# Layer norm tails rebuilt around the next stage's first products, and the first expert weights split inside the routing chain

## The reference, cut down

```
mix = hybrid_mixer(x, w_in[l], ...)                 # x @ w_in (1024 x 3088), attentions, then y @ w_out (1024 x 1024)
x = layer_norm(ALPHA * x + mix, ln1_g[l], ln1_b[l])
ffn = (silu(conv(x @ w_up)[gate]) * conv(x @ w_up)[value]) @ w_down    # 2 x 2816 columns up, 2816 rows down
x = layer_norm(ALPHA * x + ffn, ln2_g[l], ln2_b[l])

def layer_norm(x, g, b):
    mu = x.mean(-1); var = square(x - mu).mean(-1)
    return (x - mu) * rsqrt(var + 1e-5) * g + b
```

## Time and profile before

| | |
|---|---|
| median of 3 runs | 3308.24 us (3307.53 to 3309.69) |
| profiled execution, its own time | 3307.87 us |
| its span, first to last instruction | 3306.1 us |
| PE busy | 2997.5 us (91%) |
| DVE busy | 2490.6 us (75%) |
| ACT busy | 1367.0 us (41%) |
| POOL busy | 453.8 us (14%) |
| mean granted PE clock | 0.941 |

### The profile page before, as it was taken

One profiled execution on the slowest core, in us unless ns is written; L12 is line 12 of the kernel. 1 busy time (PEld: TensorE's weight loads), 2 busy tenths in 40 slices (PEclk: granted clock), 3 DMA queues, 4 the chain that ended last, 5 costly groups with the idle time before them and its releaser, 6 DMA issues. The chain is left out here.

```text
span 3306.1 us, 40370 instructions
## 1 busy us (share of the span) xinstructions
PE 2997.5 (91%) x13932; PEld 2416.0 (73%) x13932; DVE 2490.6 (75%) x2714; ACT 1367.0 (41%) x1618; POOL 453.8 (14%) x252
## 2 busy tenths in 40 slices
PE   8987999989988999879978999995998969999995
PEld 6776888867766878757767888884765767888884
DVE  4566888565568995676958999996487658999996
ACT  1241211002311110064235777773336227777774
POOL 0111113211102123300000000002323000000001
PEclk9998999989988999989988999997999979999997
DMA  4243664322324663164229999994212339999993
GB/s 165 64 160 102 194 215 153 115 106 90 140 90 141 218 202 115 39 176 120 73 111 353 373 370 374 385 362 155 90 54 84 117 137 373 378 378 388 386 385 142
DMA packets 346507, 667.25 MB, mean 202 GB/s; under 512 B 21936, under 2 KB 138604, under 8 KB 338172
## 3 DMA queue, kind: packets, MB, share of 16 engines
q1 hardware_dynamic: 339612, 642.58, 55.5%
q0 software_dynamic: 6752, 22.81, 2.0%
HBM read 612.20 MB, written 53.13 MB: 201 GB/s over the span
## 5 line engine op out<-in xcount | busy, mean ns | idle before, releaser
L2702 DVE TENSOR_TENSOR expert_w_low<-expert_w_raw,expert_w_high 128x2048 fp32r<-128x2048 f32 x290 | 663.3, 2289 | 64.9 <-ACT expert_w_high L2663 64.7
L2663 ACT CAST expert_w_high<-expert_w_raw 128x2048 fp32r<-128x2048 f32 x290 | 554.9, 1914 | 181.3 <-PE bank L144 178.3
L142 PE MATMUL bank<-expert_w_high,expert_x_high 128*128 128x512 f32 x928 | 379.5, 409 | 5.4 <-DVE expert_w_low L2702 4.5
L144 PE MATMUL bank<-expert_w_high,expert_x_low 128*128 128x512 f32 x928 | 364.8, 393 | 0.0
L142 PE MATMUL bank<-first_XH,first_w_high 128*128 128x512 f32 x912 | 363.1, 398 | 1.1 <-DVE first_w_low L221 1.1
L143 PE MATMUL bank<-expert_w_low,expert_x_high 128*128 128x512 f32 x928 | 363.7, 392 | 0.0
L143 PE MATMUL bank<-first_XL,first_w_high 128*128 128x512 f32 x912 | 357.2, 392 | 0.0
L144 PE MATMUL bank<-first_XH,first_w_low 128*128 128x512 f32 x912 | 356.8, 391 | 0.0
L221 DVE TENSOR_TENSOR first_w_low<-first_w_raw,first_w_high 128x2048 fp32r<-128x2048 f32 (+2 forms) x100 | 302.8, 3028 | 3.4
L219 DVE CAST first_w_high<-first_w_raw 128x2048 fp32r<-128x2048 f32 (+2 forms) x100 | 119.8, 1198 | 173.3 <-PE bank L144 167.8
L2535 POOL DMA_INDIRECT expert_x_rows<-h_rows,slot_token x58 | 66.2, 1142 | 1266.8 <-PE bank L2568 862.5
(11 more groups left out here) (523 smaller groups left out, 6013.2 us busy)
## 6 DMA issues: line engine op xcount, KB each, us to landing
expert_w_raw<-in_moe_w_gate_dram SPq DMA_DIRECT2D x116, 1024.0 KB, 8.3
expert_w_raw<-in_moe_w_up_dram SPq DMA_DIRECT2D x116, 1024.0 KB, 13.9
expert_w_raw<-in_moe_w_down_dram SPq DMA_DIRECT2D x58, 1024.0 KB, 13.6
modulation<-in_moe_w_down_dram SPq DMA_DIRECT2D x58, 1024.0 KB, 13.9
ffn_mod_w<-in_ada_w_dram SPq DMA_DIRECT2D x48, 1024.0 KB, 5.0
first_w_raw<-in_w_up_dram SPq DMA_DIRECT2D x88, 512.0 KB, 6.4
first_w_raw<-in_w_down_dram SPq DMA_DIRECT2D x22, 1024.0 KB, 4.9
first_w_raw<-in_w_in_dram SPq DMA_DIRECT2D x20, 1024.0 KB, 5.1
```

The costliest lines, as they stand in the source:

```text
L142: nc.tensor.matmul(out, rounded(st[0]), rounded(mv[0]), start=start, stop=False)
L144: return nc.tensor.matmul(out, rounded(st[1]), rounded(mv[0]), start=False, stop=stop)
L2663: nc.scalar.copy(rounded(high[:, part_of(e, n), :]), weights.place(place)).then_inc(w_high, 1)
L2702: nc.vector.tensor_tensor(rounded(low[:, part_of(e, n), :]), weights.place(place), high[:, part_of(e, n), :], ALU.subtract).then_inc(w_spl ...
```

## The change

**Layer norm.** A class `RowNorm` replaces both tails. The mean and the sum of squares are now taken on ACT, each by one 1024-wide activation with an accumulator (L1056 and L1060 of the new file), with a small one for the negated mean between them (L1058). DVE does two 1024-wide scalar_tensor_tensor instructions per tile, which take in gain and bias. POOL does nothing in a tail.

**Order on PE.** `last_products` replaces `last_tiles`: the transposes of tiles 0 and 1 stand before the last two product tiles. Between and behind the transposes of tiles 2 and 3 stand the next phase's first products: in `output_norm_phase` the two jobs of up slot 0, in halves of 256 tokens (`up_job`), in layer 0's `ffn_phase` the four jobs of the first half-depth slot of the next projection (`first_value_job`). The next phase skips them, and both of its first slots are split already: high parts on ACT, low parts on DVE, inside the tail. Layer 1's `ffn_phase` has the new norm alone.

**Experts.** ACT writes the first slot's high part before the second small exponential. DVE writes the first low part before the wait for `ranked`, the second before the wait for `listed`, and the third behind the rows. The second half of the first rows is transposed into bank 7.

```diff
+def last_products(slots, tile, used, turn):
+    f, l = slots - 2, slots - 1
+    if f % Weights.RING == 0:
+        tile(f, 0)
+        tile(f, 1)
+        tile(l, 0, True)
+        tile(f, 2)
+        tile(l, 1, True)
+        tile(f, 3).then_inc(used, 1)
+        rest = l
+    else:
+        tile(f, 0)
+        tile(f, 1)
+        tile(l, 0, True)
+        tile(l, 1, True)
+        tile(l, 2)
+        tile(l, 3).then_inc(used, 1)
+        rest = f
+    turn(0)
+    tile(rest, 2, True)
+    turn(1)
+    tile(rest, 3, True)
...
+    def deviation(self, act, t):
+        x, at = self.G["X"][:, t, :], slice(t, t + 1)
+        act.wait_ge(self.summed, 2 * t + 2)
...
+        self.nc.scalar.activation(self.squares, x, ACT.Identity, accum_out=self.total[:, at]).then_inc(self.total_done, 1)
...
+        self.nc.scalar.activation(self.less_mean[:, at], self.total[:, at], ACT.Identity, scale=-1.0 / D).then_inc(self.mean_done, 1)
...
+        self.nc.scalar.activation(self.squares, x, ACT.Square, bias=self.less_mean[:, at], accum_out=self.square_sum[:, at]
...
+        self.nc.scalar.activation(self.std[:, at], self.square_sum[:, at], ACT.Sqrt, scale=1.0 / D, bias=self.G["eps_ln"][:, :]
```

In `output_norm_phase`, PE:

```diff
+            row_products(nc, pe, ps, weights, acts, product_done, lambda t: norm.turn(pe, t, turned))
+            norm.turn(pe, 2, turned)
+            pe.wait_ge(next_weights.split, 1)
+            pe.wait_ge(split.low, 4)
+            up_job(nc, G, next_weights, 0, slice(0, 2 * P))
+            norm.turn(pe, 3, turned)
+            up_job(nc, G, next_weights, 1, slice(0, 2 * P))
+            pe.wait_ge(split.low, 8)
+            for i in range(2):
+                up_job(nc, G, next_weights, i, slice(2 * P, 4 * P)).then_inc(next_weights.done, 1)
```

In `ffn_phase`, PE, where a next projection exists:

```diff
+                pe.wait_ge(next_weights.split, 1)
+                pe.wait_ge(split.low, 2)
+                first_value_job(nc, G, next_weights, 0)
+                norm.turn(pe, 2, turned)
+                pe.wait_ge(split.low, 4)
+                first_value_job(nc, G, next_weights, 1)
+                norm.turn(pe, 3, turned)
...
```

In the expert phase, DVE (the two functions run before the waits for `ranked` and `listed`):

```diff
+            chain.on_vector(dve, lambda: weight(Step(0), 0), lambda: weight(Step(0), 1))
             for half in range(2):
                 rows(None, half)
+            for n in range(2, PARTS):
+                weight(Step(0), n)
```

More of the change, by code:

```diff
@@ L1043, in row_products @@
         last.then_inc(weights.used, 1)
-    for s, t in last_tiles(slots):
-        pe.wait_ge(weights.split, s + 1)
-        tile(s, t)
+    last_products(slots, tile, weights.used, turn)
 def output_norm_phase(nc, l, G, weights, g_dram, b_dram, next_weights):
@@ L1098, in stats_of @@
[L1098 to L1105, removed]
@@ L1116, in _ @@
             for s in range(1, slots):
                 weights.split_slot(dve, s)
[L1118 to L1124 removed]
+            for t in range(2):
+                norm.residual(dve, t)
+                norm.centre(dve, t)
+                norm.scale(dve, t)
+            norm.residual(dve, 2)
+            split.low_parts(dve, 0)
@@ L1126, in _ @@
+            next_weights.split_low_dve(dve, 0)
+            norm.residual(dve, 3)
+            norm.centre(dve, 2)
+            norm.scale(dve, 2)
+            split.low_parts(dve, 1)
+            norm.centre(dve, 3)
+            norm.scale(dve, 3)
+            split.low_parts(dve, 2)
+            split.low_parts(dve, 3)
+            next_weights.split_low_dve(dve, 1)
         @block.scalar
         def _(act):
-            for t in range(TT):
-                act.wait_ge(var_done, t + 1)
-                nc.scalar.activation(std[:, t:t + 1], mv[:, t, 1:2], ACT.Sqrt, bias=G["eps_ln"][:, :]).then_inc(std_done, 1)
@@ L1131, in _ @@
-            split.high_parts(act)
-        @block.gpsimd
-        def _(pool):
-            pool.wait_ge(rows_loaded, 32)
-            for t in range(TT):
-                pool.wait_ge(scaled, t + 1)
-                nc.gpsimd.tensor_tensor(X[:, t, :], X[:, t, :], b_row[:, :], ALU.add).then_inc(shifted, 1)
+            norm.deviation(act, 0)
+            norm.deviation(act, 1)
+            act.wait_ge(weights.used, slots - 1)
+            next_weights.split_high(act, 0, None)
+            split.high_part(act, 0)
@@ L2449, in expert_phase @@
         down_bank = lambda c: ps[4 + c]
+        rows_bank = lambda first, half: ps[HIDDEN_BANK if first and half else X_BANK]
         block = ph.block()
```

282 lines of the change are left out of this document (155 added, 127 removed).

## The result

The changed kernel takes 3270.66 us (median of 4 runs, 3265.62 to 3272.11) where the kernel before takes 3307.89: a ratio of 0.9883, interval 0.9871 to 0.9895. Applied to the 3308.24 of the front that is 3269.5, half a microsecond under the range of 3270 to 3289 that was forecast: 38.7 us gained where 31 were forecast. By the two medians alone the gain is 37.2 us. The profiled execution is the fastest of the four (3265.6).

A forecast was written before the change was run, and what follows sets the result against it. PE bounds the stages, so time can come only from the seams where it waits. Gains 10 + 14.2 + 3 + 3.8 = 31 us off 3307.9 give 3276.9, with 0.4 for the median 3277.3; range 3270 to 3289.

The forecast's parts named there:

- I take 5 for each of the two tails, 10 together: Both output_norm tails: new norm and next phase's products moved into the tail; worked gain 5.3 us each, taken as 5.
- job j = 1: First product job left behind the first output_norm tail's barrier: to start at 329.1, after barrier, wait for taps and transposes.
- Half products: Next phase's 256-column products in the output_norm tails, priced at 0.12 us each, 72 of them ending at 324.6.
- rival 1: Output_norm tails: halves load-bound, 0.16 to 0.236 us instead of 0.12, 3.8 to 11 us more per tail; 3285 to 3299; 10%.
- the estimate of 0.216 us: Output_norm tails: load and half product not overlapped; 96 cost 9 us more per tail, total about 3296.
- Layer 0's ffn tail: New order, norm and moved products let PE start the second half-depth slot at 715.4, not 729.6: gain 14.2 us.
- The table load: Layer 0's ffn tail: ACT's 1.28 us load now stands between tile 0's squares and root; deviation 1.3 late, PE waits 0.7.
- Layer 1's ffn tail: Only the new norm: last low part ends at 708.9 against 711.9, gain 3 us.
- Experts: Two expert phases: gather 2.0 us late, but first products at 1748.5 against 1750.42; gain 1.9 us each, 3.8 together.
- Rival 2: Transfers or DVE late at the next phase's start, 2 to 4 us in each of three places: 3283 to 3289; 10%.
- Rival 3: PE's clock recovers earlier or does not fall at the barrier, 2.3 us in up to three seams: 3268 to 3274; 12%.
- Rivals 4 and 5: Tails lengthen by what next phases save, 3301 to 3310, 4%; PE stays at 1.2 GHz in up stage, 3315 up, 2%.

The follow-up runs named there:

- splits_behind_chain: Changed kernel, but in the expert phases DVE writes the first two low parts directly behind the routing chain, not inside it: 3269.65 us, ratio 0.9877.
- taps_inside: Changed kernel, but in both ffn phases PE turns the convolution's taps inside its first job, behind 12 of its 24 products: 3276.39 us, ratio 0.9898.
- busy_wait: Changed kernel with 12 more products, result unused, at the start of each ffn phase ahead of the wait for the taps: 3271.88 us, ratio 0.988.
- early_and_taps: Changed kernel with the next phase's slot 2 requested inside the tail and the taps turned inside PE's first job: 3261.12 us, ratio 0.9853.

## Why the prediction was wrong

- **The step that failed** is the size of "I take 5 for each of the two tails, 10 together": 6.5 and 7.7 in one profile, 6.8 and 7.0 in the other. That is 4.2 of the 6.1 us by which the seams of the first profile exceed the forecast of 31, and 3.8 of the 4.6 of the second. The mechanism was right. In the first tail, with 3.1 added to the times of the new profile, tile 2's transposes were put at 309.0 and stand at 305.19 + 3.1 = 308.3; the halves' end at 324.7, and it is 323.3; job j = 1 at 329.1, and it is 328.0. The first 0.7 comes from DVE: I added busy times, and neighbours overlap.

```profile
303.85 1.28 DVE L1079 SCALAR_TENSOR_TENSOR x_tokens<-mix_out_centred,mix_out_rstd,mix_out_b_row 128x1024 f32<-128x1024 f32 x1
305.05 1.28 DVE L261 TENSOR_TENSOR first_XL<-bank,first_XH 128x512 fp32r<-128x512 f32 x2
306.25 1.28 DVE L1071 SCALAR_TENSOR_TENSOR mix_out_centred<-x_tokens,mix_out_less_mean,mix_out_g_row 128x1024 f32<-128x1024 f32 x1
```

  Rows of 1.28 start 1.20 apart, and the earlier trace rows give only their length. The eight instructions from low part 0 to tile 2's norm take 7.2 us (297.86 to 305.05), where I had 7.8. Another 0.5 comes from tile 2's transposes, which give way to the half job after 1.3 us (305.19 to 306.48) and not 1.8, since the clock rose within them. And I rounded 5.3 down to 5. In the second tail of the first profile come another 1.2. Half of it is the kernel before, which took 0.6 longer over this tail than over the first. The other half is what is left of an earlier rise of the clock (24 half products in 3.5 us, against 4.1) and a shorter wait for the taps: PE was 1.7 us ahead of the first tail by its fifth product and lost 1.1 of it again, in part in a wait of 0.5 us for slot 2.

```profile
976.94 0.56 PE L142 MATMUL bank<-first_XH,first_w_high 128*128 128x256 f32 x1
980.41 1.03 PE L1088 MATMUL bank<-ident,x_tokens 128*128 128x128 f32 x8
993.76 0.44 PE L1358 MATMUL bank<-ident,ffn_small_rows 44*128 44x44 f32 x4 [3.68 <-DMA ffn_small_rows<-in_conv_b_dram]
```

- **Half products** at 0.12: measured 0.121 at full clock. The pair of load and product takes little more than half of 0.227, so the load lies beside the products, and rival 1 falls. With it falls the estimate of 0.216 us for a pair that does not overlap, worked out from the 107 ns of a load in the Trainium skill, "TensorE: Matmul & The Clock Gate", section "LDWEIGHTS (loading the stationary operand)".
- **Layer 0's ffn tail**: 14.2 forecast, 15.3 measured; the first product behind the barrier at 714.2 on the time axis of the kernel before (704.61 + 9.6), not 715.4. Same cause: the 15 us of DVE work from residual 2 to the last low part were summed by their lengths to 16. The table load stands where it was put, and PE waits 0.33 us behind it, not 0.7:

```profile
675.59 1.28 ACT L1063 ACT_TABLE_LOAD   x1
676.88 0.30 ACT L1063 ACTIVATE ffn_std<-ffn_square_sum,eps_ln 128x1 f32<-128x1 f32 x1
```

- **Layer 1's ffn tail**: 3 forecast, 3.2 and 3.3 measured. **Experts**: 3.8 forecast; 4.4, 3.2 and, alone, 3.6 measured. But one step in it was wrong in size: counted from the router's first row, the gather was issued 1.4 us later than before and its rows were turned 1.0 us later in the first phase of the first profile (1.0 to 1.7 in the four of both profiles), not 2.0. And the chain's waits were no good place for the low parts, as splits_behind_chain shows.
- **Rival 2** (transfers late at the next phase) was nearer than its 10%: I found "1 to 2 us of room" for up slot 2; there was none. PE waits 0.3 and 0.5 us for it in two of the four tails of the two profiles. What taps_inside and busy_wait let PE start earlier was lost there, until slot 2 was requested earlier. Projection slot 2 kept its room: DVE had split it at 714.08, and no row of PE there carries a wait. **Rival 3** (the clock rises earlier) shows in two of these four tails: the 11 intervals behind the taps take 4.0 and 4.2 us there, 4.8 and 4.9 in the others. But its price was worked out wrong: 2.3 us in one to three seams below 3277.3 is 3270.4 to 3275.0, not 3268 to 3274. **Rivals 4 and 5** did not come.
- **The range** ended at 3270 because only rival 3 led below the forecast; the sum itself, made of lengths that erred to the slow side, had no bound of its own downward. Both ways of reading the result lie within 0.7 us of that end.
- **Open**: how much of the second output_norm tail's 7.7 and 7.0 us is the change. Against the shorter execution of the old tail (1.6 us) they are 6.1 and 5.4, and the tails' excess over the 10 is 2.6 and 2.2 us. Why the clock rose earlier in one execution than in another is not shown.

## What to carry to other kernels

Sum what DVE does in a row by the distances between starts, not by the lengths of its rows: over a tail of 15 us the lengths were 1 us too long, always to the same side. When a seam is shortened, look at once for the transfer that is requested behind it: here two edits that each brought nothing, or lost 6 us, brought 9 together. Products of the next phase that need only half the rows fill the waits of a tail well; the norm and the splits alone did not move an output_norm tail. And profile the kernel before more than once: one of its seams differed by 1.6 us between two executions.

## What the hardware showed that was not expected

- Pauses of PE of 1.0, 1.5 and 1.6 us left its clock at the upper level (0.227 to 0.236 us a product of 512 columns behind them), as did the 2.81 of the earlier trace rows, whose transposes still take 1.09. Behind pauses of 3.7 to 4.4 us the lower level came, at once or after some products: the first 11 intervals took 4.0 to 4.9 us.
- How soon the clock rises again differs between executions of one program: the same 24 half products took 3.5 to 4.3 us in the two profiles of the changed kernel.
- POOL's low part of 2048 columns took 4.61 us beside DVE's work, and DVE's rows, each of which reads a bank, kept their length (0.69) meanwhile.
- DVE's low part of a slot, which reads two operands from `first_w_raw` and `first_w_high`, did not keep its length beside POOL. In the profile of the changed kernel 34 of its 94 low parts of 2048 columns have no row of POOL beside them, and all of these take 2.3 us; the 60 that have one take 3.3 or 4.4. Two of up slot 2, in taps_inside and in early_and_taps, and POOL's row beside the latter:

```profile
336.97 2.29 DVE L222 TENSOR_TENSOR first_w_low<-first_w_raw,first_w_high 128x2048 fp32r<-128x2048 f32 x1
333.39 3.27 DVE L222 TENSOR_TENSOR first_w_low<-first_w_raw,first_w_high 128x2048 fp32r<-128x2048 f32 x1
332.37 2.13 POOL L1540 TENSOR_TENSOR ffn_hidden<-ffn_gate,ffn_conv 128x512 f32<-128x512 f32 x1 [7.20 <-DVE ffn_conv L1480]
```
